# The last 64-slot expert pass stands step by step between the steps of the last 128-slot pass

## The chip, the cores and the metric

One core of a Trainium2 chip runs the whole kernel. The metric is device time in microseconds. A core has PE (the matrix engine, TensorE), DVE (VectorE), ACT (ScalarE), POOL (GpSimd) and SP (SyncE, which here only issues DMAs), and 16 DMA engines that bring data from HBM.

## What is computed

A two-layer encoder trunk on 256 tokens of 1024 columns, all float32. Layer 0 is dilated attention and a dense SwiGLU; layer 1 is grouped-query attention and a top-2-of-8 mixture of experts. The change touches the mixture alone:

```python
def moe_swiglu(h, router_w, w_gate, w_up, w_down):
    logits = (h @ router_w).astype(jnp.float32)
    top_val, top_idx = lax.top_k(logits, TOP_K)
    top_w = jax.nn.softmax(top_val, axis=-1)
    gates = jnp.sum(jax.nn.one_hot(top_idx, N_EXPERTS, dtype=jnp.float32) * top_w[..., None], axis=-2)
    y = jnp.zeros_like(h)
    for e in range(N_EXPERTS):
        y = y + gates[..., e:e + 1] * swiglu(h, w_gate[e], w_up[e], w_down[e])
    return y
```

`w_gate` and `w_up` are 1024 x 3584 for each expert, `w_down` is 3584 x 1024: 42 MiB an expert, 336 MiB in all, each byte fetched once.

## The kernel before, in words

**Passes.** Experts are ordered by how many tokens chose them. Each is a pass over its own slots: the tokens of an expert are gathered into 64 or 128 columns by a product with a 0/1 matrix, go through the SwiGLU, and are scattered back to the 256 tokens, weighted, by a product with the turned gate matrix (`SgT`). `PASSES` has six passes before the loop: five with 64 slots, kind S (places 0, 2, 3, 4, 5, here S0, S2 to S5), and the wide one, kind L (place 1, 128 + 64 slots). Two passes with 128 slots, kind M, follow: the one in a loop (here M6; the loop runs `loops` times, once with this data) and the last (here M7). Place 5 is the last S.

**Steps and tiles.** A pass has NF = 7 steps of 512 hidden columns. A step has six tiles of 1 MiB: two of gate weights, two of up, two of down. M7.2 is step 2 of M7. The downs of a step are done one step later, so a step is: gates, turning of the step before's hidden values, ups, downs of the step before.

**Two ways to multiply.** In a 64-slot step (`gate_beside_up`, `down_halves`) the tiles are multiplied as they landed, in float32, with gate and up beside each other in the two column halves of the array. In 128-slot and wide steps a tile is split: ACT makes the rounded high part (`high`, into one of three `whi`), DVE the rest (`low`, `wlo`), and PE adds three fast products per block (`tile_products`; it waits for high, then for low). The hidden values are split in the same way (`hidden_high` on ACT, `hidden_low` on DVE).

**Order.** `units()` lists the steps up to M6: the seven steps of S0, then S2 to S5 with the parts G, U and D (gates, ups, downs) of the seven wide steps put in behind the S steps that `WIDE_AFTER` names. All engines follow this list, each in order; within an S step, `middles` and `lates` name what else stands before and behind the second gate/up pair: gathers, turned gates, and pieces. A piece is one quarter of a scatter, taken through bank 6 of PSUM and added to `yacc` by DVE. Those of S5 (`piece`, L1729) also hold the wide expert's two parts, from `SgTl`, `yea` and `yeb`. Then comes the loop (`expert_pass`), and `expert_pass(..., True)` for M7; its own scatter stands behind its last downs.

**DMA.** SP issues the tiles in the order of use. A tile waits until its buffer is free (`raw_free`): for a split tile when `low` is done (`lo_done`), for one taken whole when PE has used it (`w_used`). There are six buffers (`RAW`), and two more while `RING_OF_8` holds (in the mix of S and wide steps). In an M step the two down tiles are asked for in the order second, first, once the buffer of the second is free (`e_down`, L627):

```python
raw_free(s + 1 - RAW, rr)
for k in (1, 0):
```

Of the kernel before, what the change touches and what calls it, by code (L numbers as in the profile page):

```python
# [38 lines left out]
NE = 8  # L39
# [44 lines left out]
WIDE_AFTER = ((0, 1, 2), (4, 5, 6), (8, 9, 10), (12, 13, 14), (15, 16, 17), (18, 19, 20), (21, 22, 23))  # L84
# [17 lines left out]
UNITS = units()  # L102

# [19 lines left out]

def small(q, i):
# [4 lines left out]
def small_before(q, i):  # L129

    if i:
        return q, i - 1
    return (max(q - 1, 0) if q > 2 else 0, NF - 1) if q else None
# [17 lines left out]
def as_landed():  # L151

    whole = set()
    for n, unit in enumerate(UNITS):
# [3 lines left out]
        elif unit[0] == "M":  # L158
            whole.update((s + 4, s + 5))
    return whole  # L160
# [3 lines left out]
SPLIT = [s for s in range(tile_of(NE + 1, 0) + 6 * NF) if s not in WHOLE]  # L164
# [15 lines left out]
def in_buffers():  # L180

    last, came, earlier = {}, {}, {}
    for s in range(tile_of(NE + 1, 0) + 6 * NF):
# [17 lines left out]
def split_before(s):  # L201

    return s - SPL if s >= LOOPED else SPLIT[split_at(s) - SPL]
# [48 lines left out]
def build(nc, dram, out):  # L252
    ctx = ExitStack()
    with ctx:
# [88 lines left out]

        rw = sb("rw", [P, KC, NE])
# [131 lines left out]
        tail_hidden = sem("tail_hidden")  # L476
        tb_done = sem("tb_done")
# [69 lines left out]
        def _(sp):  # L547
# [123 lines left out]
            for unit in UNITS:  # L671
# [16 lines left out]
                else:  # L688
                    e_gate(chosen[q], i, s, 0)
                    e_up(chosen[q], i, s + 2, 0)  # L690
                    e_down_static(chosen[FIRST_M - 1], NF - 1, s + 4, True)
            sp.wait_ge(w_used, FIRST_TILE["M", FIRST_M, 0])
# [8 lines left out]
            expert_tiles(FIRST_M, e, None, NF * loops)  # L701
# [29 lines left out]
        def _(act):  # L731
# [327 lines left out]
            def small_step(n, q, i, middle=None):  # L1059
# [12 lines left out]
                if w is not None:  # L1072
# [3 lines left out]
                    act.activation(hhb[:, :, 0:HP], tail_h, ACT.Copy).then_inc(bhi_done, 1)  # L1076
                following = UNITS[n + 1]
# [33 lines left out]
            def expert_pass(q, p=0, final=False):  # L1111
                rr = NF * p
                aside = {}
                if not final:
                    aside[5] = lambda: evacuate_gathers(q + 1, 2, p)
                    aside[6] = lambda: high_again(p, tile_of(q, 6), rr)
                for i in range(1, NF):
                    step(q, i, (q, i - 1), rr, 5 if final and i == NF - 1 else 6, aside.get(i))
                if final:
                    hidden_high(NHALF + steps_a(q) + NF - 1 + rr)  # L1120
                    gate_row(3)
                    act.wait_ge(w_used, tile_of(q + 1, 0) + 2 + 6 * rr)
                else:
                    step(q + 1, 0, (q, NF - 1), rr)
# [1513 lines left out]
```

## Time and profile before

| | |
|---|---|
| median of 3 runs | 1679.59 us (1675.41 to 1681.35) |
| profiled execution | 1682.09 us, span 1680.4 us |
| PE busy | 1623.3 us, 97% |
| DVE, ACT busy | 891.2 us (53%), 682.7 us (41%) |
| DMA | 504.78 MB, mean 300 GB/s |
| granted TensorE clock, mean | 0.983 |
| experts | 741 to 1666 us of the span |

The page gives busy time by engine and groups of instructions by source line; PE's products overlap, so that each record is longer than the distance to the next one (0.39 us against 0.23 us for 512 columns). A step's length is therefore read from start to start. DMA shares are means over 16 engines and can read a little over 1.

### The profile page before, as it was taken

The numbers are of one execution on the slowest core, as the hardware profiler recorded it, in microseconds if no ns is written. First come the engines' busy times: TensorE is split into PE (matmuls) and PEld (weight loads), VectorE is DVE, ScalarE is ACT, GpSimd is POOL, SyncE is SP. The second block draws the span as 40 slices with busy tenths as digits, with TensorE's granted clock in tenths as the row PEclk, the third lists the DMA queues.
The fourth block names the chain that finished last, engine by engine and source line by source line (L and its number), as shares of the span: only waits on it lengthen the run. The fifth ranks groups of instructions, "written<-read, shape, count | busy, mean of one in ns | idle before, by whom it ended". The sixth has DMA issues, their size and how long they took to land.

```text
span 1680.4 us, 23999 instructions
## 1 busy us (share of the span) xinstructions
PE 1623.3 (97%) x9497; PEld 1176.6 (70%) x9497; DVE 891.2 (53%) x989; ACT 682.7 (41%) x823; POOL 50.2 (3%) x100
## 2 busy tenths in 40 slices
PE   5999999999999999999899999999999999999997
PEld 4999999789999977753454545555555545788785
DVE  5666667667776679521133223233323225888786
ACT  2444445553333356520221322222232314667674
POOL 0200000001111000000000000000000000000000
PEclk9999999999999999979999999999999999999999
DMA  9986556248888633059999999999999999989993
GB/s 347 349 258 226 192 198 220 71 154 308 306 298 303 230 115 133 30 212 368 398 394 399 396 378 398 390 398 387 383 362 367 398 385 378 384 329 330 367 354 126
DMA packets 236641, 504.78 MB, mean 300 GB/s; under 512 B 11360, under 2 KB 83200, under 8 KB 227584
## 3 DMA queue, kind: packets, MB, share of 16 engines
q1 hardware_dynamic: 221264, 458.26, 74.6%
q0 software_dynamic: 12032, 43.00, 7.1%
q10 hardware_dynamic: 3248, 2.17, 0.4%
q8 instruction: 68, 1.11, 0.3%
q14 instruction: 29, 0.24, 0.0%
HBM read 502.34 MB, written 1.05 MB: 300 GB/s over the span
## 4 chain that ended last, share of the span: by engine, by line
PE 88%; DVE 5%; DMA 3%; ACT 2%; issue 1%; ACTq 0%; SPq 0%; DVEq 0%
PE ps L1618 15%; PE ps L1567 14%; PE ps L1168 10%; PE ps L1172 9%; PE ps L1175 9%; PE ps L1571 8%; PE ps L1631 7%; PE ps L1549 2%; PE ps L1655 1%; PE ps L1740 1%; PE ps L1261 1%; PE ps L1223 1%; DMA raw<-l_exp_w_up 1%; DVE wlo L1925 1%; DMA raw<-l_exp_w_down 1%
## 5 line engine op out<-in xcount | busy, mean ns | idle before, releaser
L1925 DVE TENSOR_TENSOR wlo<-raw,whi 128x2048 fp32r<-128x2048 f32 x210 | 476.7, 2288 | 221.3 <-ACT whi L740 216.7
L740 ACT ACTIVATE whi<-raw 128x2048 fp32r<-128x2048 f32 x210 | 398.9, 1910 | 147.0 <-PE ps L1172 80.5
L1168 PE MATMUL ps<-ahi,whi 128*128 128x256 f32 x832 | 239.1, 287 | 1.7 <-DVE alo L1993 1.7
L1172 PE MATMUL ps<-alo,whi 128*128 128x256 f32 x832 | 236.2, 284 | 0.0
L1175 PE MATMUL ps<-ahi,wlo 128*128 128x256 f32 x832 | 236.0, 284 | 0.0
L1618 PE MATMUL ps<-raw,arena 128*64 128x512 f32 x768 | 179.2, 610 | 7.4 <-DMA raw<-l_exp_w_up 5.3
L1168 PEld LDWEIGHTS ps<-ahi,whi 128*128 128x128 f32 x832 | 160.3, 193 | 5.1 <-issue 3.8
L1172 PEld LDWEIGHTS ps<-alo,whi 128*128 128x128 f32 x832 | 160.5, 193 | 0.3
L1175 PEld LDWEIGHTS ps<-ahi,wlo 128*128 128x128 f32 x832 | 160.4, 193 | 0.0
L2499 DVE TENSOR_TENSOR arena<-arena,ps 128x256 f32<-128x256 f32 x35 | 14.7, 421 | 273.9 <-ACT arena L1051 273.9
L1567 PE MATMUL ps<-whi,alo 128*128 128x512 f32 x448 | 156.6, 390 | 0.0
L1567 PE MATMUL ps<-whi,ahi 128*128 128x512 f32 x336 | 135.3, 403 | 0.0
L1618 PEld LDWEIGHTS ps<-raw,arena 128*64 128x64 f32 x768 | 53.1, 139 | 111.5 <-issue 106.4
L1168 PE MATMUL ps<-whi,ahi 128*128 128x256 f32 (+1 forms) x352 | 109.5, 311 | 2.5 <-DVE alo L1993 2.5
L1172 PE MATMUL ps<-whi,alo 128*128 128x256 f32 (+1 forms) x352 | 107.2, 305 | 0.0
L1175 PE MATMUL ps<-wlo,ahi 128*128 128x256 f32 (+1 forms) x352 | 107.1, 304 | 0.0
L1051 ACT ACTIVATE arena<-ps 128x256 f32<-128x256 f32 x35 | 13.4, 382 | 227.0 <-PE ps L1655 227.0
L1571 PE MATMUL ps<-wlo,ahi 128*128 128x512 f32 x336 | 103.6, 390 | 0.0
L1631 PE MATMUL ps<-raw,arena 128*64 128x512 f32 x448 | 101.6, 595 | 0.0
L1567 PEld LDWEIGHTS ps<-whi,alo 128*128 128x128 f32 x448 | 84.2, 188 | 18.0 <-issue 1.0
L1938 DVE SCALAR_TENSOR_TENSOR acc<-mod_raw,ccol,acc 128x1024 f32<-128x1024 f32 x70 | 89.6, 1280 | 0.9
L1567 PEld LDWEIGHTS ps<-whi,ahi 128*128 128x128 f32 x336 | 63.1, 188 | 27.1 <-issue 10.8
(296 smaller groups left out, 2333.2 us busy)
## 6 DMA issues: line engine op xcount, KB each, us to landing
raw<-l_exp_w_down SPq DMA_DIRECT2D x96, 1024.0 KB, 9.5
raw<-l_exp_w_up SPq DMA_DIRECT2D x88, 1024.0 KB, 11.0
raw<-l_exp_w_gate SPq DMA_DIRECT2D x86, 1024.0 KB, 9.3
raw<-l_w_in SPq DMA_DIRECT2D x42, 1024.0 KB, 6.5
mod_raw<-mod_w POOLq DMA_DIRECT2D x80, 512.0 KB, 5.8
mod_raw<-l_exp_w_gate SPq DMA_DIRECT2D x23, 1024.0 KB, 8.5
dist_gb<-l_exp_w_up SPq DMA_DIRECT2D x22, 1024.0 KB, 10.7
raw<-l_ffn_w_gate SPq DMA_DIRECT2D x14, 1024.0 KB, 5.1
```

What stands on the lines that cost most here:

```text
L740: act.activation(whi[n % SPL][:, :], landed_in(s), ACT.Copy).then_inc(hi_done, 1)
L1168: pe.matmul(dst, stat[0], mov[0], start=start, stop=False, skip_group_check=True)
L1172: hi = pe.matmul(dst, *cross[0], start=False, stop=False, skip_group_check=True)
L1175: return pe.matmul(dst, *cross[1], start=False, stop=stop, skip_group_check=True)
L1223: ins = pe.matmul(bank(b, kc, kc + 1), acc[:, kc * P:(kc + 1) * P], ones[:, 0:1], start=True, stop=True)
L1549: ins = pe.matmul(ps[:, b * BANK + kc * n:b * BANK + (kc + 1) * n], xo[:, tt, kc * P:(kc + 1) * P], sel[:, tt, :], start=(tt == 0), stop=( ...
L1567: ins = pe.matmul(dst, stat, whi[n % SPL][:, a:a + BANK], start=start, stop=False, skip_group_check=True)
L1571: ins = pe.matmul(dst, stat, wlo[n % SPL][:, a:a + BANK], start=False, stop=stop, skip_group_check=True)
L1618: ins = pe.matmul(half_bank(1, half), slots_of(q)[:, kc, :], landed_in(s + half)[:, kk * BANK:kk * BANK + BANK], start=kc == 0, stop=kc == ...
L1631: ins = pe.matmul(half_bank(0, half), sb_h[:, fc, :], landed_in(s)[:, at:at + BANK], start=i == 0 and fc == 0, stop=i == NF - 1 and fc == ...
L1925: dve.tensor_tensor(wlo[n % SPL][:, :], landed_in(s), whi[n % SPL][:, :].bitcast(F32), ALU.subtract).then_inc(lo_done, 1)
L1938: dve.scalar_tensor_tensor(acc[:, :], src, c, acc[:, :], ALU.mult, ALU.add).then_inc(mod_used, 1)
```

## The change

1. S5 leaves the list of units. S2 to S4 are followed by M6 at once, and `WIDE_AFTER` packs the wide parts behind the steps of three passes: the wide step 4's downs (D) and the wide step 5's gates (G) stand behind the same S step. The middles and lates are dealt out anew.
2. M7 becomes `final_pass`: a list FINAL with M7.1, S5.0, M7.2, S5.1, ..., M7.6, S5.5, then the downs of M7.6 (D), S5.6 and the downs of S5.6 (E). S5 computes in banks 3 and 2. The pieces that hold the wide expert now also hold M6's scatter and stand in S5.1 and S5.2. M6 scatters S4.
3. At the end the scatter products of M7 stand before the last downs of S5, and those of S5 (64 rows each, from `last_SgT` and `last_ye` in `mod_raw`) behind them, into the same four banks.
4. Eight buffers hold for 192 tiles instead of 240. From M6 on there are six, as before.

```diff
-WIDE_AFTER = ((0, 1, 2), (4, 5, 6), (8, 9, 10), (12, 13, 14), (15, 16, 17), (18, 19, 20), (21, 22, 23))
+LAST_S = 5
+WIDE_AFTER = ((0, 1, 2), (3, 4, 5), (6, 7, 8), (9, 10, 11), (12, 13, 14), (14, 15, 16), (17, 18, 19))
...
-    for n in range(NF * (FIRST_M - 2)):
+    for n in range(NF * (LAST_S - 2)):
...
+FINAL = [u for i in range(1, NF) for u in (("M", i), ("S", i - 1))] + [("D", NF - 1), ("S", NF - 1), ("E", NF - 1)]
...
-RING_OF_8 = range(AHEAD.stop, AHEAD.stop + 8 * 30)
+RING_OF_8 = range(AHEAD.stop, AHEAD.stop + 8 * 24)
...
+                if kind == "M":
+                    raw_free(EARLIER[s + 5], rr)
+                    for k in (1, 0):
+                        sp.dma_start(landed_in(s + 4 + k).rearrange("p (k n) -> p k n", k=2),
+                                     rows_256(e, i - 1, k, False)).then_inc(landed[buffer_of(s + 4 + k)], 16)
...
+                    if kind == "M":
+                        high(s + 3, rr)
+                        silu(f + i, s + 2 + 6 * rr)
+                        high(s + 4, rr)
+                        hidden_high(f + i - 1)
+                        high(s + 5, rr)
+                    if kind == "S":
+                        if i:
+                            small_silu(LAST_S, i - 1)
...
+                        act.wait_ge(w_used, s + 4 + 6 * rr)
+                        act.activation(sb_g, bank(3), ACT.Copy).then_inc(gu_copied, 1)
...
+                        for j in range({"M": SPL, "D": 2}.get(following[0], 0)):
+                            high(FINAL_TILE[following] + j, rr)
+                small_silu(LAST_S, NF - 1)
+                act.wait_ge(w_used, TILES + 6 * rr)
+                act.activation(last_ye[0:HP, :], half_bank(2, 0), ACT.Copy).then_inc(last_out, 1)
...
+                middles = {1: lambda: joint_piece(0), 2: lambda: joint_piece(2), 3: last_gates, 5: last_hidden}
+                lates = {1: lambda: joint_piece(1), 2: lambda: joint_piece(3), 5: lambda: spread_gate(3)}
...
+                    elif kind == "S":
+                        if i:
+                            pe.wait_ge(gu_copied, small(LAST_S, i))
+                        gate_beside_up(LAST_S, s, 0, 3, rr)
+                        if i:
+                            beside_T(small(LAST_S, i))
+                        if i in middles:
+                            middles[i]()
+                        gate_beside_up(LAST_S, s + 2, 1, 3, rr)
+                        if i in lates:
+                            lates[i]()
+                        if i:
+                            small_downs(LAST_S, i - 1, s + 4, 2, rr)
...
+                for j in range(4):
+                    pe.matmul(sums[j], SgT[:, j // 2 * P:j // 2 * P + P], ye[:, j % 2 * BANK:j % 2 * BANK + BANK],
+                              start=True, stop=False, skip_group_check=True)
+                small_downs(LAST_S, NF - 1, FINAL_TILE["E", NF - 1], 2, rr)
+                pe.wait_ge(last_out, 2)
+                for j in range(4):
+                    rows = slice(j % 2 * HP, j % 2 * HP + HP)
+                    pe.matmul(sums[j], last_SgT[rows, j // 2 * P:j // 2 * P + P], last_ye[rows, :],
+                              start=False, stop=True, skip_group_check=True).then_inc(scat, 1)
...
-            expert_pass(FIRST_M, loops, True)
-            pe.wait_ge(y_add, 4 * (FIRST_M - 1 + loops) + 1)
-            scatter(FIRST_M + 1, 0, 2, loops)
-            pe.wait_ge(gb_done, 4)
-            scatter(FIRST_M + 1, 1, 4, loops, False)
+            final_pass(loops)
```

Three places show how instructions now stand. DVE between the wide steps 4 and 5, before: low halves of two down tiles, four adds of wide sums, the hidden values of the next 64-slot step, a copy of turned gates, then the low halves of the next two wide tiles.

```order
L2514 TENSOR_TENSOR hhb<-mod_raw,hhb 128x4x64
L1925 TENSOR_TENSOR wlo<-raw,whi 128x2048 x2
L2491 TENSOR_TENSOR arena<-arena,ps 128x512 x4
L2499 TENSOR_TENSOR arena<-arena,ps 128x256
L2483 COPY arena<-ps 128x256
L1925 TENSOR_TENSOR wlo<-raw,whi 128x2048 x2
```

The same place after:

```order
L2648 TENSOR_TENSOR hhb<-mod_raw,hhb 128x4x64
L2057 TENSOR_TENSOR wlo<-raw,whi 128x2048 x2
L2625 TENSOR_TENSOR arena<-arena,ps 128x512 x4
L2057 TENSOR_TENSOR wlo<-raw,whi 128x2048 x2
L2633 TENSOR_TENSOR arena<-arena,ps 128x256
```

The 64-slot step that stood between the adds and the next gates' low halves stands behind them.

ACT in M7, around the end of a step, before: silu of the gates (L911), high parts (L740) and the hidden values' high part (L915).

```order
L534 REGISTER_ALU [waits w_used]
L911 ACTIVATE arena<-ps 128x512 [waits h_ready]
L534 REGISTER_ALU [waits landed4]
L740 ACTIVATE whi1<-raw4 128x2048 [waits lo_done,hi_used]
L914 REGISTER_ALU
L915 ACTIVATE hhi<-ps 128x512 [waits t_done]
L534 REGISTER_ALU [waits landed5]
L740 ACTIVATE whi2<-raw5 128x2048 [waits lo_done,hi_used]
L737 REGISTER_ALU
L534 REGISTER_ALU [waits landed0]
L740 ACTIVATE whi0<-raw0 128x2048 [waits lo_done,hi_used]
```

After, at the end of an M step and in the S step behind it (L1104 is the S step's silu, L1195 the copy of its gates):

```order
L968 ACTIVATE hhi<-ps 128x512 [waits t_done]
L559 REGISTER_ALU [waits landed3]
L793 ACTIVATE whi2<-raw3 128x2048 [waits lo_done,hi_used]
L1104 ACTIVATE arena<-ps 128x256 [waits tb_done]
L1194 REGISTER_ALU
L1195 ACTIVATE arena<-ps 128x512 [waits w_used]
L790 REGISTER_ALU
L559 REGISTER_ALU [waits landed4]
L793 ACTIVATE whi0<-raw4 128x2048 [waits lo_done,hi_used]
```

The high part of the next M step's first tile now stands behind the copy of the S step's gates, which waits for PE (`w_used`).

SP in M7, a step's ups and downs and the next step's gates, before:

```order
L563 DMA raw2<-l1_exp_w_up 128x4x512 [waits lo_done]
L534 REGISTER_ALU
L563 DMA raw3<-l1_exp_w_up 128x4x512 [waits lo_done]
L534 REGISTER_ALU
L632 ISA [waits lo_done]
L632 DMA raw5<-l1_exp_w_down 128x2x1024
L632 ISA
L632 DMA raw4<-l1_exp_w_down 128x2x1024
```

After, M7.2, the step behind S5.0:

```order
L588 DMA raw5<-l1_exp_w_gate 128x4x512
L576 REGISTER_ALU
L588 DMA raw0<-l1_exp_w_up 128x4x512 [waits w_used]
L576 REGISTER_ALU
L588 DMA raw1<-l1_exp_w_up 128x4x512 [waits w_used]
L576 REGISTER_ALU
L746 ISA [waits w_used]
L746 DMA raw3<-l1_exp_w_down 128x2x1024
L746 ISA
L746 DMA raw2<-l1_exp_w_down 128x2x1024
```

The buffers of these tiles came free with a split before; now they come free when PE has used the S step's tiles.

## Rows read from the trace of the kernel before

**Rows 1.** Busy by stretch: us; PE, PEld, DVE, ACT, POOL busy; clock; DMA share, GB/s.

```profile
859.10:1407.20 548.10, 548.10 (x2533) 280.53 (x2532) 160.31 (x198) 139.47 (x179) 0.00 (x0) 1.00 1.02 387
1407.20:1441.10 33.90, 32.48 (x146) 24.41 (x145) 26.19 (x16) 22.98 (x18) 0.00 (x0) 1.00 0.98 372
1441.10:1549.20 108.10, 108.10 (x499) 88.61 (x498) 92.49 (x60) 77.33 (x57) 0.00 (x0) 1.00 0.93 343
1549.20:1569.90 20.70, 18.63 (x77) 14.95 (x76) 15.60 (x9) 13.81 (x10) 0.00 (x0) 0.92 1.01 381
1569.90:1665.60 95.70, 95.67 (x435) 77.70 (x434) 77.80 (x50) 63.06 (x42) 0.00 (x0) 1.00 0.79 296
```

**Rows 2.** Waits of PE, 859 to 1666 us: us in total, times, longest.

```profile
PE ps L1567 <- DVE hlo L2125: 3.5, 2, 2.1
```

**Rows 3.** DMA in the mix, 800 to 1120 us.

```profile
DMA packets 49432, 125.84 MB, mean 393 GB/s; under 512 B 1918, under 2 KB 1918, under 8 KB 45318
```

**Rows 4.** Timeline of PE, a 64-slot step: start, us, engine, line.

```profile
1351.11 0.75 PE L1655 MATMUL ps<-cst,arena 128*128 128x128 f32 x4
1351.79 3.65 PE L1618 MATMUL ps<-raw,arena 128*64 128x512 f32 x16
1355.27 3.60 PE L1631 MATMUL ps<-raw,arena 128*64 128x512 f32 x16
1358.71 3.60 PE L1618 MATMUL ps<-raw,arena 128*64 128x512 f32 x16
1362.24 0.74 PE L1655 MATMUL ps<-cst,arena 128*128 128x128 f32 x4
```

**Rows 5.** Timeline of PE, the same place in two 128-slot steps running.

```profile
1520.98 0.60 PE L1398 MATMUL ps<-cst,arena 128*128 128x128 f32 x4
...
1537.82 0.60 PE L1398 MATMUL ps<-cst,arena 128*128 128x128 f32 x4
```

**Rows 6.** Chain that ended last, M6.1: start us, us, what.

```profile
1422.74 0.37 SPq L632
...
1423.31 6.92 DMA raw<-l_exp_w_down
...
1430.38 0.05 ACT whi L740
...
1435.55 1.65 PE ps L1567 x6
```

**Rows 7.** The same chain, M7.1.

```profile
1550.10 7.34 DMA raw<-l_exp_w_down
...
1562.79 3.42 PE ps L1567 x8
```

**Rows 8.** Stretches behind three holes of PE: columns as in rows 1.

```profile
802.50:808.00 5.50, 5.50 (x20) 2.02 (x21) 0.00 (x0) 0.00 (x0) 0.00 (x0) 0.73 1.05 402
1435.60:1440.00 4.40, 4.40 (x20) 3.62 (x20) 4.40 (x3) 2.69 (x2) 0.00 (x0) 1.00 1.05 387
1562.80:1567.20 4.40, 4.40 (x12) 3.48 (x13) 4.40 (x3) 1.75 (x2) 0.00 (x0) 0.61 1.06 390
```

**Rows 9.** Instructions by line and form: busy us, mean ns; idle before.

```profile
L1925 DVE TENSOR_TENSOR wlo<-raw,whi 128x2048 fp32r<-128x2048 f32 x119 | 268.7, 2287 | 97.1 <-ACT whi L740 97.1
L740 ACT ACTIVATE whi<-raw 128x2048 fp32r<-128x2048 f32 x119 | 225.5, 1912 | 52.5 <-PE ps L1567 37.7 <-DMA raw<-l_exp_w_gate 5.4 <-DMA raw<-l_exp_w_up 4.5
...
L1071 ACT ACTIVATE arena<-ps 128x512 f32<-128x512 f32 x35 | 20.9, 596 | 118.1 <-PE ps L1618 118.1
...
L2491 DVE TENSOR_TENSOR arena<-arena,ps 128x512 f32<-128x512 f32 x24 | 15.4, 683 | 24.3 <-PE ps L1582 15.6 <-PE ps L1588 8.7
```

**Rows 10.** Chain at the end, behind the last downs.

```profile
1665.57 1.16 issue
1666.73 3.69 PE ps L1707 x8
```

**Rows 11.** Timeline of ACT, a half-height copy.

```profile
1424.48 0.59 ACT L1057 ACTIVATE arena<-ps 64x512 f32<-64x512 f32 x1
```

More of the change, by code:

```diff
@@ L121, in tile_of, with final_tiles @@
     return FIRST_TILE["M", FIRST_M, 0] + 6 * (NF * (q - FIRST_M) + i)
+def final_tiles():
+    at, s = {}, tile_of(FIRST_M + 1, 1)
+    for unit in FINAL:
+        at[unit] = s
+        s += 2 if unit[0] in "DE" else 4 if unit == ("S", 0) else 6
+    return at, s
+FINAL_TILE, TILES = final_tiles()
 def small(q, i):
@@ L182, in in_buffers @@
     last, came, earlier = {}, {}, {}
-    for s in range(tile_of(NE + 1, 0) + 6 * NF):
+    for s in range(TILES):
         b = buffer_of(s)
@@ new lines, in final_pass, with joint_add, last_gates @@
+            def final_pass(loops):
+                rr, f = NF * (loops - 1), NHALF + steps_a(FIRST_M) + NF * loops
+                def joint_add(j, b):
+                    tt, n = j % 4 // 2, j % 2
+                    dve.wait_ge(y_add, 13 + 4 * loops + j)
+                    dve.wait_ge(scat, 12 + 4 * loops + j + 1)
+                    part_y = yacc[:, tt, n * BANK:n * BANK + BANK]
+                    dve.tensor_tensor(part_y, part_y, b, ALU.add).then_inc(y_add, 1)
+                def last_gates():
+                    dve.wait_ge(selT, FIRST_M + 1 + loops)
+                    dve.tensor_copy(SgT, bank(6, 0, NT * P)).then_inc(selT_e, 1)
+                middles = {1: lambda: joint_add(0, bank(6)), 2: lambda: (joint_add(2, bank(6)), choose(loops, True)),
+                           3: last_gates, 5: lambda: hidden_low(f + NF - 1, bank(6))}
+                lates = {1: lambda: joint_add(1, bank(6)), 2: lambda: joint_add(3, bank(6))}
+                for n, unit in enumerate(FINAL):
+                    (kind, i), s = unit, FINAL_TILE[unit]
+                    if kind == "M":
+                        low(s + 3, rr)
+                        low(s + 4, rr)
+                        hidden_low(f + i - 1, bank(6))
+                        low(s + 5, rr)
+                        hidden(f + i, s + 4 + 6 * rr)
+                    elif kind == "S":
+                        if i:
+                            small_hidden(LAST_S, i - 1)
+                        if i in middles:
+                            middles[i]()
+                        if i in lates:
+                            lates[i]()
+                        following = FINAL[n + 1]
+                        for j in range({"M": SPL, "D": 2}.get(following[0], 0)):
+                            low(FINAL_TILE[following] + j, rr)
+                small_hidden(LAST_S, NF - 1)
+                dve.wait_ge(w_used, TILES + 6 * rr)
+                dve.tensor_copy(last_ye[HP:P, :], half_bank(2, 1)).then_inc(last_out, 1)
+                for j, b in enumerate((4, 5, 0, 1)):
+                    joint_add(4 + j, bank(b))
```

275 lines of the change are left out of this document (168 added, 107 removed).

## The prediction, written before the changed kernel ran

> **What bounds the kernel now.** I read the stretches first, then the waits, then single steps. From 859 us to 1407 us (the mix: 64-slot passes S2 to S5 with the wide expert) PE is busy for 548.10 of 548.10 us, at full clock, while DMA moves 387 GB/s; in the next 258 us (the two 128-slot passes, M6 in the loop and M7 behind it) PE is full but for two holes, and DMA falls to 343 and 296 GB/s [rows 1]. The list of PE's waits over both says the same: two waits, 3.5 us in all, the longer 2.1 us [rows 2]. So PE's product stream sets the time from 859 to 1666 us, and DMA is close behind it in the mix: 393 GB/s is what it moves when it is always full [rows 3], which makes 2.67 us of a 1.049 MB tile, 16.0 us of the six tiles of a step.
>
> Two periods matter. A 64-slot step takes PE 11.13 us (transposes to transposes, 1351.11 to 1362.24: 0.68 transposes, 3.48 second gate/up pair, 3.44 downs, 3.53 first pair of the next step) [rows 4]. A 128-slot step takes 16.84 us (1520.98 to 1537.82) [rows 5]. Against 16.0 us of DMA the one eats DMA's lead and the other just keeps it.
>
> **What the change can't give.** The listing of PE's instructions holds the same products in the same shapes, in another order: 7 steps of S5 and the four three-part pieces leave the mix and stand in M7, the scatter of M7 stands ahead of the last downs instead of behind. PE is the full engine on both sides, so moving is worth nothing by itself; only holes in PE count. The change wins what holes it closes and loses what it opens.
>
> **The old holes stay.** The 1.4 us hole is in M6's second step. Its chain: the pair of down tiles is asked for at 1422.74, when the 64-slot downs free their buffers, the tile that is used first lands second at 1430.23, it is split, the hidden values' low half waits behind that on VectorE, and PE starts at 1435.55 [rows 6]. The 2.1 us hole is the same chain at the loop's end: 7.34 us from issue to landing, products at 1562.79 [rows 7]. Neither edge is touched by the change (S4 stands where S5 stood). What each holds: about 7.5 us from the request of a down pair to the landing, 5.3 us from the landing to PE's downs. Behind the second hole the granted clock reads 0.61 over 4.4 us (a part at 1.2 instead of 2.4 GHz), 1.7 us lost; behind the first it stays at 1.00; behind an earlier hole, at 802 us, it reads 0.73 over 5.5 us [rows 8]. I take 1.7 us for holes of 2.1 us and more, nothing for shorter ones.
>
> **New holes, one by one.** (Mk.i is step i of a 128-slot pass, Sk.i of a 64-slot pass.)
>
> 1. *Wide step 4 runs straight into wide step 5's gates.* PE waits for VectorE to add all four wide sums; after the last downs two adds of 0.683 us are left [rows 9], with 0.2 us of handing over: 1.6 us, once. Between 0 (if the adds were done) and 2.8 us (all four late); I take 1.6. Clock stays.
>
> 2. *S5.0 into M7.2.* ScalarE stands in order: it copies the gates of the 64-slot step (0.60 us) and only then makes the high half of the next 128-slot tile (1.91 us) [rows 9]. In every other 64-slot step small downs (3.44 us) cover this. S5.0 has none, so PE waits 0.60 + 1.91 + 0.1 = 2.6 us, then 0.4 us more for VectorE's low half (2.29 us against eight high products, 1.8 us). With the clock's 1.7: 4.7 us. Bounds 2.6 and 4.7.
>
> 3. *S5.1 into M7.3, S5.2 into M7.4.* The down pair of the 128-slot step may be asked for only when the 64-slot downs before it end; that is the hole of rows 6 again, 1.4 us each: 2.8 us, clock kept. The two pieces of 2.7 us in these steps give DMA time.
>
> 4. *S5.3 into M7.5, S5.4 into M7.6.* Here the queue itself is late. With six buffers (the mix has eight) nothing can be fetched ahead until the first gate/up pair of the 64-slot step is used; then six tiles must come, 16.0 us, and the one that is used first comes last, 2.0 us of latency on top (7.34 less two tiles) and 0.3 us to issue: landed 18.3 us after the pair, PE's downs ready 5.3 us later, at 23.6. PE's own way from there: 0.68 + 3.48 + 3.44 to the end of the 64-slot step, then 11.4 us to the 128-slot downs (16.84 less 5.44 of downs), 19.0 us in S5.4; the transposes of the last gates make it 19.4 in S5.3. Holes of 4.6 and 4.2 us, each with 1.7 us of clock: 12.2 us. Lower bound: the same at 403 GB/s and no clock loss, 8.0; upper, at 375 GB/s, 14.
>
> 5. *Entry to M6* is fetched in the last steps of S4 with six buffers, and the gather for M6 stands one step closer to it: ScalarE and VectorE finish about as PE arrives. 0.2 us, between 0 and 1.5.
>
> 6. *The end.* Before, PE stood 1.16 us after the last downs for a copy of 1024 columns, then did four scatter products in 3.69 us [rows 10]. Now the copy is half as high and half as wide, 0.59 us on each of two engines [rows 11], 0.71 with handing over: 0.45 us gained. The four products are as many, with 64 rows each. I take no gain of them (0 to 1.8 us).
>
> The Trainium skill, TensorEngine Tiling, section Overview, has it that products contracting 64 rows can run side by side in two halves of the array. For column halves the trace shows it: 16 records of half width end in 3.65 us. For row halves no run here shows it; by that rule the end would be half of 3.69 us, 1.8 us, shorter.
>
> What hides the rest: routing, choosing and gate work that moves on VectorE and ScalarE lies in the mix, where VectorE is busy for 160 and ScalarE for 139 of 548 us [rows 1]. SyncE's one more register load falls where it waits for a buffer.
>
> **Sum.** 1.6 + 4.7 + 2.8 + 12.2 + 0.2 - 0.45 = +21.0 us. The profiled execution took 1682.09 us, its span 1680.4 and 1.7 around it; it would take 1703.1. It lies 2.5 us above the median of the three runs, 1679.59; from the median the sum gives 1700.6, so 1701.
>
> **Rivals.**
>
> *DMA's lead carries (no change).* The mix now has three light 64-slot steps to each wide step where it had four, so DMA gets further ahead in it, and if M7 starts with all buffers full and the down pairs land in time, items 3 and 4 vanish. Left are 1.6 + 2.6 + 0.4 (no clock loss) - 0.45 - 0.5 = +3.7 us: 1683. Against it: a lead is capped by six buffers, and rows 6 show the hole right behind a full mix.
>
> *PE isn't the bound (faster).* If PE's busy share only hid waiting for data, DMA would be the bound, and filling it in the 128-slot passes would pay. The bytes there, 372 x 33.9 + 343 x 108.1 + 381 x 20.7 + 296 x 95.7, are 85.9 MB, at 393 GB/s 219 us instead of 258 [rows 1, 3]: up to 40 us, 1640. It decides at the first step where PE is full and could start earlier. Against it: PE's steps have the same length with DMA at 387 and at 296 GB/s, and nobody is named in its waits. A smaller form of it (the two old holes close, 3.5 + 1.7 us, and the end gives 2) lands at 1674.
>
> The Trainium skill, Perfetto Trace Analysis, section Identifying the Most-Contended Engine, holds matmul busy time to be a bad measure and wants the weight loads' share; the section Optimization Strategy says that interleaving regimes with different bounds may help. Weight loads are busy for 281 of 548 us in the mix and 89 of 108 us in M6 [rows 1]; by that rule PE has headroom in the mix and this rival holds, 1640 to 1674. I follow the rows on PE's waits.
>
> *M7 is bound by DMA all through (slower still).* If DMA's round trips leave each of the five edges from a 64-slot into a 128-slot step as item 4 has it, items 3 grow from 1.4 to 6.3 us each: +31 us, 1711. It decides when the pieces of S5.1 and S5.2 don't lengthen the way enough: 2 x 2.7 us against a hole of 4.6, so they should.
>
> **Chances and numbers.** The forecast 0.72 (its own range 1690 to 1709: no clock losses and 403 GB/s at one end, 375 GB/s and the late entry at the other); lead carries 0.10; faster 0.09; bound by DMA throughout 0.09. A measurement of this kernel tells about 0.3%, 5 us, from no change. Faster 0.09, same 0.10, slower 0.81. The range takes in the forecast and the case that the lead carries: 1683 to 1710.
>
> **What would show it.** In the changed kernel's trace: PE's steps of 11.1 and 16.8 us as before; a hole of about 1.6 us where wide downs meet wide gates; a wait of PE for the high half, some 2.6 us, after the 64-slot step that has no downs; then waits for the hidden values' low half, short ones in M7.3 and M7.4, 4 us in M7.5 and M7.6, each led by the landing of a down tile, with DMA near 393 GB/s across M7. I am wrong if PE's product stream in the mix gets shorter than its steps add up to (then it wasn't the bound), if the holes of M6.1 and M7.1 are gone (the lead does carry), or if M7.5 and M7.6 show none.

## The result and the profile of the changed kernel

| | kernel before | changed kernel |
|---|---|---|
| time, median of the runs side by side | 1679.99 us (4 runs) | 1705.72 us (4 runs, 1702.80 to 1709.61) |
| ratio to before | | 1.0163, 95% interval 1.0143 to 1.0182 |
| profiled execution, its span | 1682.09, 1680.4 us | 1702.80, 1701.1 us |

The change costs 25.7 us (1.6%). The forecast was 1701 in a range of 1683 to 1710, slower with a chance of 0.81. The sign and the size came out (the sum was 21.0 us), the size in part by luck: some of its terms were wrong, in opposite directions, and offset each other.

The page of the changed kernel, busy time by engine:

```profile
span 1701.1 us, 24069 instructions
PE 1625.0 (96%) x9497; PEld 1172.5 (69%) x9497; DVE 890.6 (52%) x986; ACT 680.5 (40%) x822; POOL 50.2 (3%) x100
```

The same stretches as in [rows 1]: the mix, M6, M7.1, and M7.2 to the end of the last downs, by each engine's busy time, granted clock, DMA share and GB/s:

```profile
851.50:1312.30 460.80, 459.42 (x2144) 249.26 (x2144) 154.34 (x187) 130.86 (x163) 0.00 (x0) 1.00 0.96 362
1312.30:1459.80 147.50, 143.10 (x645) 114.64 (x644) 119.43 (x75) 101.20 (x75) 0.00 (x0) 0.98 0.96 354
1459.80:1476.90 17.10, 17.10 (x79) 13.66 (x77) 11.68 (x7) 8.72 (x7) 0.00 (x0) 1.00 1.04 393
1476.90:1686.80 209.90, 194.66 (x823) 110.45 (x822) 85.39 (x58) 74.17 (x59) 0.00 (x0) 0.97 0.92 346
```

DMA now moves 346 GB/s where M7 moved 296 before, and nothing came of it: PE has 15 us of holes in that stretch. PE's waits from 860 us to the end of the downs name them (us in total, times, longest), where [rows 2] had two waits and 3.5 us:

```profile
PE ps L1646 <- DVE hlo L2257: 16.9, 6, 4.6
PE ps L1646 <- ACT whi L793: 2.5, 1, 2.5
PE ps L1646 <- DVE arena L2625: 1.4, 1, 1.4
PE ps L1650 <- DVE wlo L2057: 0.2, 1, 0.2
```

L1646 and L1650 are the 128-slot products (L1567 and L1571 before), L2257 makes the low half of the hidden values, L793 the high half of a weight tile, L2625 adds the wide sums. Stretch by stretch, measured from PE's start of a step to its start of another:

| stretch | before | after | difference |
|---|---|---|---|
| start to the mix (S0, S1, routing) | 838.39 | 830.82 | -7.6, not by the change |
| mix, to M6.0 | 568.89 | 481.50 | -87.4 |
| M6, to M7.1 | 141.93 | 147.46 | +5.5 |
| M7.1 | 20.73 | 17.09 | -3.6 |
| M7.2 to the end of the downs | 95.63 | 209.96 | +114.3 |
| end | 14.83 | 14.27 | -0.6 |

The first line holds none of the changed code; it varies between executions (24 us at the lower clock around 724 us in the one profile, 3.4 in the other). From the mix on the change costs 28.2 us in these two profiles. The medians of the whole time differ by 25.7, and the two spans alone (20.7 apart) would have told a story that is too short.

### The profile page after: what moved, and what is told of

Same layout as the page of the kernel before. It is cut to its first block, busy times and chain, and to the rows that moved or that the text cites. A ratio compares the mean times of both kernels' runs of the same rounds, so it can differ in the third digit from the quotient of the medians.

```text
span 1701.1 us, 24069 instructions
## 1 busy us (share of the span) xinstructions
PE 1625.0 (96%) x9497; PEld 1172.5 (69%) x9497; DVE 890.6 (52%) x986; ACT 680.5 (40%) x822; POOL 50.2 (3%) x100
## 2 busy tenths in 40 slices
DMA packets 236643, 504.78 MB, mean 297 GB/s; under 512 B 11361, under 2 KB 83201, under 8 KB 227585
## 4 chain that ended last, share of the span: by engine, by line
PE 85%; DVE 5%; DMA 5%; ACT 2%; issue 2%; SPq 0%; ACTq 0%; DVEq 0%
PE ps L1697 14%; PE ps L1646 13%; PE ps L1247 10%; PE ps L1251 9%; PE ps L1254 9%; PE ps L1650 7%; PE ps L1710 7%; DMA raw<-l_exp_w_down 3%; PE ps L1628 2%; PE ps L1734 1%; PE ps L1340 1%; PE ps L1302 1%; ACT whi L793 1%; DMA raw<-l_exp_w_up 1%; DVE wlo L2057 1%
## 5 line engine op out<-in xcount | busy, mean ns | idle before, releaser
L2057 DVE TENSOR_TENSOR wlo<-raw,whi 128x2048 fp32r<-128x2048 f32 x218 | 495.1, 2289 | 245.2 <-ACT whi L793 240.2
L793 ACT ACTIVATE whi<-raw 128x2048 fp32r<-128x2048 f32 x218 | 412.7, 1909 | 151.8 <-PE ps L1251 80.5
L1697 PE MATMUL ps<-raw,arena 128*64 128x512 f32 x720 | 165.6, 603 | 7.7 <-DMA raw<-l_exp_w_up 5.2
L1646 PE MATMUL ps<-whi,alo 128*128 128x512 f32 x448 | 156.8, 390 | 0.0
L1646 PE MATMUL ps<-whi,ahi 128*128 128x512 f32 x336 | 135.4, 403 | 3.9 <-ACT whi L793 2.5
L1697 PEld LDWEIGHTS ps<-raw,arena 128*64 128x64 f32 x720 | 49.1, 137 | 103.3 <-issue 98.7
L1710 PE MATMUL ps<-raw,arena 128*64 128x512 f32 x528 | 120.0, 596 | 0.0
L1104 ACT ACTIVATE arena<-ps 128x256 f32<-128x256 f32 x35 | 13.4, 383 | 242.2 <-PE ps L1734 242.2
L1650 PE MATMUL ps<-wlo,ahi 128*128 128x512 f32 x336 | 104.5, 392 | 0.2 <-DVE wlo L2057 0.2
L1646 PEld LDWEIGHTS ps<-whi,alo 128*128 128x128 f32 x448 | 84.2, 188 | 17.6 <-issue 0.5
L1697 PE MATMUL ps<-mod_raw,arena 128*64 128x512 f32 x192 | 87.4, 598 | 0.0
```

Of the source, the lines that this page charges most:

```text
L793: act.activation(whi[n % SPL][:, :], landed_in(s), ACT.Copy).then_inc(hi_done, 1)
L1646: ins = pe.matmul(dst, stat, whi[n % SPL][:, a:a + BANK], start=start, stop=False, skip_group_check=True)
L1650: ins = pe.matmul(dst, stat, wlo[n % SPL][:, a:a + BANK], start=False, stop=stop, skip_group_check=True)
L1697: ins = pe.matmul(half_bank(b, half), slots_of(q)[:, kc, :], landed_in(s + half)[:, kk * BANK:kk * BANK + BANK], start=kc == 0, stop=kc == ...
L1710: ins = pe.matmul(half_bank(b, half), sb_h[:, fc, :], landed_in(s)[:, at:at + BANK], start=i == 0 and fc == 0, stop=i == NF - 1 and fc == ...
L2057: dve.tensor_tensor(wlo[n % SPL][:, :], landed_in(s), whi[n % SPL][:, :].bitcast(F32), ALU.subtract).then_inc(lo_done, 1)
```

## The experiments

The theory by now: PE is the bound everywhere from the mix to the end, the products are conserved, and the 26 us are holes, each made by a tile or a copy that comes late, with the lower clock behind the long ones. The rivals: DMA sets the time in M7 and PE's busy share hides it; a hole that is closed is handed on (closing one opens the next); products in this order cost PE more by themselves.

**1. The down pair in the order of use.** Both down tiles of a 128-slot step wait for the second buffer, and the one used first is fetched second. The edit turns the pair round and, from the second step of a pass on, gives each tile its own wait (`downs` takes the rows in the same order; the loop's `e_down` is edited alike):

```diff
-                    raw_free(EARLIER[s + 5], rr)
-                    for k in (1, 0):
+                    if i == 1:
+                        raw_free(EARLIER[s + 5], rr)
+                    for k in (0, 1):
+                        if i > 1:
+                            raw_free(EARLIER[s + 4 + k], rr)
                         sp.dma_start(landed_in(s + 4 + k).rearrange("p (k n) -> p k n", k=2),
-                                     rows_256(e, i - 1, k, False)).then_inc(landed[buffer_of(s + 4 + k)], 16)
+                                     rows_256(e, i - 1, 1 - k, False)).then_inc(landed[buffer_of(s + 4 + k)], 16)
```

> The changed kernel, but in every 128-slot step the down tile that is used first is also fetched first, and from the second step of a pass on each of the two waits for its own buffer alone. Theory 'late pair' (the holes come from the down pair: asked for when the 64-slot downs end, the tile used first landing last): the tile used first lands 2.7 us earlier. The hole in M6.1 falls from 4.4 to about 1.7 us and its clock loss of 1.8 goes; the holes in M7.3 and M7.4 (1.5, 1.4) vanish; those in M7.5 and M7.6 fall from 4.6 and 4.5 to about 1.8 us without clock loss. In all 15 to 19 us less than the changed kernel: about 1689 us, within 0.6% of the kernel before. Rival 'bytes' (M7 is bound by DMA's rate as a whole, the order inside only shifts where PE waits): less than 4 us, 1702 or more, with holes of the same sum elsewhere in M7.

Measured: 1692.83 us (median of 5 runs), ratio 1.0086 (1.0056 to 1.0116), half of the loss gone. PE's waits over the same stretch:

```profile
PE ps L1652 <- ACT whi L799: 5.2, 3, 2.5
PE ps L1652 <- DVE hlo L2263: 5.2, 3, 1.9
PE ps L1652 <- DVE arena L2631: 1.4, 1, 1.4
PE ps L1656 <- DVE wlo L2063: 0.6, 3, 0.2
```

The waits for the hidden values' low half fall from 16.9 us to 5.2 (M6.1, M7.5 and M7.6, none over 1.9); those of M7.3 and M7.4 are gone. M7.2's 2.5 us stays, and M7.5 and M7.6 now also wait a little at their gates. So five of the holes were the late down pair. The time came out 4 us above the forecast, which had no room for those gate waits (2.7 us in the list) nor for what M6.1, M7.5 and M7.6 kept.

**2. The highs of M7.2 ahead of the copy.** ScalarE makes the high halves for M7.2 before it copies the gates of S5.0:

```diff
+                        following = FINAL[n + 1]
+                        if i == 0:
+                            for j in range(SPL):
+                                high(FINAL_TILE[following] + j, rr)
                         act.wait_ge(w_used, s + 4 + 6 * rr)
                         act.activation(sb_g, bank(3), ACT.Copy).then_inc(gu_copied, 1)
...
-                        following = FINAL[n + 1]
-                        for j in range({"M": SPL, "D": 2}.get(following[0], 0)):
+                        for j in range({"M": SPL, "D": 2}.get(following[0], 0) if i else 0):
```

> The changed kernel, but in S5.0 ScalarE makes the three high parts for M7.2 before it copies the 64-slot step's gates. Theory 'place in ScalarE's line': PE's wait for the high part at M7.2 (2.5 us, with 0.2 and 0.45 us of small waits behind it) vanishes, 3 us less than the changed kernel, about 1703 us; the holes behind it may grow by a part of that, since PE comes to them earlier. Rival 'tile late' (the gate tile of M7.2 has not landed): the wait stays at 2.5 us, now named by the DMA.

Measured: 1708.96 us (4 runs), ratio 1.0201 (1.0160 to 1.0243): no gain. The wait for the copy is gone from the list:

```profile
PE ps L1649 <- DVE hlo L2260: 20.9, 6, 4.8
```

But these waits have grown from 16.9 us to 20.9: PE's wait at M7.2's own downs was 0.5 us in the changed kernel and is 4.5 here (the 4.8 of the list is M7.5's). The chain that ended last there (start us, us, what):

```profile
1483.96 0.37 SPq L746
...
1484.82 9.75 DMA raw<-l_exp_w_down
...
1494.72 0.05 ACT whi L793
...
1499.77 3.77 PE ps L1649 x8
```

The down pair is asked for at the end of S5.0 in any case; PE reaches the downs 3 us earlier and waits there instead, long enough to get the lower clock (eight products in 3.77 us). M7.2's 2.5 us was a cover for the late pair. This is the second rival, "handed on", and for this one hole it holds. The time was forecast at 1703 us, since the hole behind was to grow by a part only.

**3. The kernel before with six buffers ahead of M6.** The loop (from M6.1 on) runs with six buffers. By the numbers in the code (`RING_OF_8.stop` against the first tile of the loop) the ring of eight ends 4 tiles ahead of it before the change and 10 ahead of it after; it can only be cut in pieces of 24 tiles, so the smallest cut in the kernel before puts its end 28 tiles ahead. The edit does that alone:

```diff
-RING_OF_8 = range(AHEAD.stop, AHEAD.stop + 8 * 30)
+RING_OF_8 = range(AHEAD.stop, AHEAD.stop + 8 * 27)
```

> The kernel before, but the two extra buffers end 24 tiles earlier, 22 tiles ahead of M6, so that the last steps before M6 have six buffers, as the changed kernel has them from 4 tiles ahead of M6. Theory 'six buffers at the entry' (M6.1's hole grew from 1.4 to 4.4 us because the tiles of M6.0 and M6.1 are asked for late): the hole in M6.1 grows to 3 us or more, with 1.7 us of clock, and PE may wait in S5 too: 4 to 12 us slower than the kernel before, 1684 to 1692 us. Rival 'gather and routing stand one step closer to M6' (a matter of the new order, not of buffers): the hole stays at 1.4 us, 1680 us.

Measured: 1685.08 us (10 runs), ratio 1.0036 (1.0017 to 1.0055). The chain of M6.1, where [rows 6] had 6.92 us from issue to landing:

```profile
1422.44 0.37 SPq L632
...
1423.00 10.61 DMA raw<-l_exp_w_down
...
1433.76 0.05 ACT whi L740
...
1438.92 3.35 PE ps L1567 x7
```

And of the changed kernel:

```profile
1327.78 0.37 SPq L657
...
1328.35 10.18 DMA raw<-l_exp_w_down
...
1338.68 0.05 ACT whi L793
```

The pair is asked for at the same place of PE's work and lands 3.3 to 3.7 us later, behind tiles that were asked for late. With six buffers SyncE can't ask for M6's tiles in time: in the changed kernel it issues nothing from 1292.3 to 1308.5 us:

```profile
1289.68 2.59 SPq L588 DMA_DIRECT2D raw<-l_exp_w_gate  x2
1308.46 0.93 SPq L588 DMA_DIRECT2D raw<-l_exp_w_up  x2
```

These are M6.0's up tiles, 3.9 us ahead of M6.0's first product. In experiment 3 they are asked for 3.9 us ahead of it too, in the kernel before 10.7 us. So six buffers ahead of M6 are enough to make this hole with all steps in their old order, and 5.5 of the 28 us are of this kind. The cut tested is longer than the change's (28 tiles for 10), and the size is the same, 4.4 us; that 10 alone do it is the reading of the queue, not a run.

**4. A seventh buffer from S5.0 on**, in the second half of the array that the ring of eight used:

```diff
+SEVEN = FINAL_TILE["S", 0]
...
     if s in AHEAD:
         return RAW + s - AHEAD.start
+    if s >= SEVEN:
+        turn = (s - SEVEN) % 7
+        return (SEVEN - 7 + turn) % RAW if turn else 2 * RAW - 2
...
```

> The changed kernel with a seventh buffer from S5.0 on, a half of mod_raw that is free there; the down pair is fetched in the old order. Theory 'late pair': the seventh buffer lets each tile be asked for one tile earlier: M7.3 and M7.4 lose their holes (the pair waits for a gate/up pair and the first small-down tile instead of the last), M7.5 and M7.6 lose 2.7 us each and their clock loss: 10 to 13 us less than the changed kernel, about 1694 us; M6.1 stays at 4.4 us. Rival 'bytes': M7's holes keep their sum, 1704 us.

Measured: 1701.44 us (4 runs, 1694.11 to 1704.16), ratio 1.0149 (1.0112 to 1.0186). The forecast of 1694 was missed: by time it can't be told from the changed kernel. Its trace (the run of 1694.11, the fastest of the four) shows part of the forecast: M7.3 and M7.4 have no hole, M7.6's shrinks to 2.5 us without low clock, but M7.5 keeps 4.1 us and its low clock. My reading, not tested, is that one buffer more is not enough for a queue that is six tiles behind.

**5. The order of use in the kernel before.** The edit of experiment 1 on the kernel before (`e_down` and `downs`):

```diff
-                raw_free(s + 1 - RAW, rr)
-                for k in (1, 0):
-                    src = dram["l1_exp_w_down"][bass.ds(e, 1), bass.ds(i * 512 + 256 * k, 256), :]
+                if i == 0:
+                    raw_free(s + 1 - RAW, rr)
+                for k in (0, 1):
+                    if i:
+                        raw_free(s + k - RAW, rr)
+                    src = dram["l1_exp_w_down"][bass.ds(e, 1), bass.ds(i * 512 + 256 * (1 - k), 256), :]
...
-                            fc, a = 2 * k + kk, kk * D + n * BANK
-                            first, last = i == 0 and fc == 0, i == NF - 1 and fc == 3
+                            fc, a = 2 * (1 - k) + kk, kk * D + n * BANK
+                            first, last = i == 0 and k == kk == 0, i == NF - 1 and k == kk == 1
```

> The kernel before, with one edit: in every 128-slot step the down tile that is used first is asked for first, each of the two as soon as its own buffer is free, where before both waited for the second buffer. Theory (the old holes are late down pairs): the tile that is used first lands 2.7 us and more earlier, the holes of M6.1 (1.4 us) and M7.1 (2.1 us and 1.7 us of clock) close, 5 us less: 1675 us, ratio 0.997. If the holes only shrink as that of M6.1 did in the changed kernel (from 4.4 to 1.9), half of it: 1677. Rival (the holes are set by VectorE's low half, however early the tile comes): 1680, both holes still in the trace.

Measured: 1673.90 us (12 runs) beside 1677.71 (23 runs of before), ratio 0.9978 (0.9961 to 0.9994). It is the one version here that beats both kernels, by 0.2%. All that is left in its list of PE's waits over the same stretch is the wait at the very end:

```profile
PE ps L1710 <- issue: 1.2, 1, 1.2
```

Both old holes and the low clock are gone (3.5 and 1.7 us by the profile; 3.8 us by the medians).

**6. The three edits together, in the changed kernel** (those of experiments 1, 2 and 4).

> The changed kernel with the three edits together: down pair in the order of use, the highs of M7.2 ahead of the copy of the gates, a seventh buffer from S5.0 on. Theory (every new hole is a late tile or a late copy, and nothing else was lost): from 1693 us with the pair order alone, M7.2's wait (2.5 us) and what was left at M7.5 and M7.6 (four short waits, some 4 us in all) close; the entry's 1.9 us and the wide sums' 1.4 us stay: 1686 us, ratio 1.004. Rival (a wait that is closed is handed on to the next late tile, as M7.2's was when it was closed alone): 1692 us or more. Rival 2 (products interleaved this way cost more on PE by themselves): holes gone, time still above 1695.

Measured: 1686.15 us (10 runs), ratio 1.0047 (1.0029 to 1.0066), the time that the theory had. PE's waits:

```profile
PE ps L1659 <- DVE hlo L2270: 4.5, 3, 1.9
PE ps L1659 <- DVE arena L2638: 1.4, 1, 1.4
PE ps L1659 <- ACT whi L803: 0.9, 1, 0.9
PE ps L1663 <- DVE wlo L2070: 0.2, 1, 0.2
```

7.0 us of waits are left, 3.5 more than in the kernel before, and it is still 8 us behind that by the medians, 7.1 from the mix on in the two profiles. So some 4 us are not in the list; they come up again below. The waits at M7.5 and M7.6 were to close and only shrank, from 6.4 us in experiment 1 to 3.8, so this part of the theory holds in part only. With the pair order in place the edit of experiment 2 does pay: M7.2 has no hole.

**7. The pair order and the seventh buffer only.**

> The changed kernel with the down pair in the order of use and the seventh buffer, without the edit at M7.2's highs. Theory (the three edits close different holes): M7.2's 2.5 us stay, the short waits at M7.5 and M7.6 go: 1689 us, 3 above the kernel with all three. Rival (the two edits close the same holes, so the second adds nothing to the first): 1693 us, as with the pair order alone.

Measured: 1688.76 us (4 runs), ratio 1.0080 (1.0053 to 1.0107), 2.6 above experiment 6, with M7.2's 2.5 us in the trace and 3.3 us of short waits still at M7.5 and M7.6. The intervals of the two overlap, so this rests on the trace.

**8. Less data for S5.** From S5.1 on, the gate and up tiles bring a quarter of their rows and the down tiles half:

```diff
+            def part(s, src, dims):
+                raw_free(EARLIER[s], rr)
+                sp.dma_start(landed_in(s).rearrange("p (k n) -> p k n", k=dims[0])[:, 0:1, :],
+                             src[:, 0:1, :]).then_inc(landed[buffer_of(s)], 16)
...
-                    if kind == "S":
+                    if kind == "S" and i:
+                        part(s + 2 * k, expert_half("l1_exp_w_gate", last, k, i * 512), (4, 512))
+                        part(s + 2 * k + 1, expert_half("l1_exp_w_up", last, k, i * 512), (4, 512))
+                    elif kind == "S":
...
-                        fetch(s + 4 + k, rr, rows_256(last, i - 1, k, True), (2, D))
+                        part(s + 4 + k, rows_256(last, i - 1, k, True), (2, D))
```

> The changed kernel, with less data for the steps 1 to 7 of S5 that stand in M7: each gate and up tile brings a quarter of its rows (the other rows keep what the buffer held) and each down tile half. The products and copies are as many as before; S5's output is not the reference's. Some 29 MB less is moved in M7, 75 us at 393 GB/s. Theory (PE is the bound and DMA sets only the holes): PE's steps keep their 11.1 and 16.8 us; the holes of M7.5 and M7.6 (4.6 and 4.5 us, 1.7 us of clock behind each) shrink to the 1.4 us that M7.3 and M7.4 have, since the down pair is still asked for when the 64-slot downs end, or go; M6.1 and M7.2 stay: 1696 us (1692 to 1698), ratio 1.010. Rival (DMA is the bound in M7 and PE's busy time hides it): the time falls by tens of us, to 1630 to 1660.

Measured: 1707.51 us (4 runs), ratio 1.0177 (1.0147 to 1.0208). Both forecasts were wrong. The pages of the two runs have 504.78 and 479.62 MB, so the edit takes out 25 MB, not the 29 of the expectation, and it gained nothing. PE's waits still have M7.5's and M7.6's holes:

```profile
PE ps L1654 <- DVE hlo L2265: 17.2, 6, 4.5
```

DMA around M7.5, in stretches of 4 us (columns as in [rows 1]):

```profile
1584.00:1588.00 4.00, 4.00 (x24) 1.59 (x20) 0.00 (x0) 0.13 (x1) 0.00 (x0) 1.00 0.02 4
1588.00:1592.00 4.00, 4.00 (x21) 1.42 (x22) 0.76 (x2) 0.54 (x2) 0.00 (x0) 1.00 0.85 286
1592.00:1596.00 4.00, 4.00 (x20) 1.62 (x17) 1.36 (x1) 2.81 (x3) 0.00 (x0) 1.00 1.05 389
1596.00:1600.00 4.00, 4.00 (x18) 2.94 (x17) 3.23 (x2) 3.21 (x2) 0.00 (x0) 1.00 1.06 394
1600.00:1604.00 4.00, 4.00 (x21) 3.30 (x20) 3.07 (x2) 2.45 (x3) 0.00 (x0) 1.00 1.03 409
1604.00:1608.00 4.00, 2.89 (x13) 2.06 (x11) 1.51 (x1) 1.67 (x1) 0.00 (x0) 1.00 0.96 358
1608.00:1612.00 4.00, 0.61 (x3) 0.54 (x4) 3.63 (x3) 2.53 (x3) 0.00 (x0) 1.00 0.05 13
```

DMA stands nearly still, at 4 GB/s, in the 4 us ahead of 1588, then is full for 18 us, then stands still again, while PE waits. Those 18 us are the 128-slot step's own six tiles, which none of the lightened tiles are; they can be asked for only when the 64-slot step's first pair gives its buffers free. What I had lightened was the wrong half. For the rival "DMA is the bound" the run is decisive all the same: with 25 MB less and DMA idle for whole stretches, the time stays.

**9. Less data for M7**, the mirror of it: the gate and up tiles of M7.2 to M7.6 bring a quarter of their rows, all else is whole.

```diff
-                        fetch(s + k, rr, expert_half("l1_exp_w_gate", e, k, i * 512), (4, 512))
+                        part(s + k, expert_half("l1_exp_w_gate", e, k, i * 512), (4, 512))
...
-                if kind == "M":
+                if kind == "M" and i > 1:
+                    for k in range(2):
+                        part(s + 2 + k, expert_half("l1_exp_w_up", e, k, i * 512), (4, 512))
+                elif kind == "M":
```

> The changed kernel, with less data for the 128-slot steps 2 to 7 of M7: each gate and up tile brings a quarter of its rows (the other rows keep what the buffer held), the down tiles are whole, S5's tiles are whole. The products and copies are as many as before; M7's output is not the reference's. It is the mirror of the run that lightened S5's tiles and left the holes of M7.5 and M7.6 as they were, with DMA full for just the 18 us of the 128-slot step's own six tiles (1588 to 1606 us there) and nearly idle ahead of them. Theory (the holes are the round trip of those six tiles, asked for only when the 64-slot step's first pair is used): with 4 of them at a quarter (0.67 us each for 2.67) the pair lands 7.5 us after the 64-slot downs end, as in M7.3; PE's holes at M7.5 and M7.6 shrink from 4.6 and 4.5 us to 1.4 or less and their low clock goes, M6.1 and M7.2 stay: 1697 us (1694 to 1699), ratio 1.011. Rival (the holes are set by the two down tiles alone, whatever comes ahead of them): holes of 4 us and more, 1704 to 1708 us.

Measured: 1693.10 us (6 runs, 1688.80 to 1700.88), ratio 1.0058 (1.0039 to 1.0077); its profiled execution is one of the longer ones, 1698.92. PE's waits:

```profile
PE ps L1654 <- DVE hlo L2265: 10.4, 5, 4.4
PE ps L1654 <- ACT whi L801: 2.5, 1, 2.5
```

The 4.4 is M6.1, which isn't touched. M7.5's hole is 2.1 us and M7.6's 1.3, where it was 4.6 and 4.5. The forecast was 1.4 or less and no lower clock for both; M7.5's is longer and keeps 3.4 us of it. The down pair before M7.5 now lands in 7.36 us instead of 10.21, and PE starts 12.6 us behind its issue:

```profile
1594.65 7.36 DMA raw<-l_exp_w_down
...
1607.23 2.98 PE ps L1654 x8
```

That is [rows 7]'s round trip again, so what is left is the late request, as in M7.3. The median lies 4 us under the forecast, the profiled execution 2 above it.

## Why the prediction was right

Its reading of the bound held. The mix became shorter by 87.4 us. By the prediction's own lengths, seven steps of 11.13 us and four pieces of 2.7 us leave it, 88.7, and a hole of 1.6 comes in: 87.1. PE's steps keep their length wherever no hole is in them, but for some 0.5 us a round in M7 (below). The rule on weight loads that it set against the rows, from the Trainium skill, Perfetto Trace Analysis, section Identifying the Most-Contended Engine, would have PE with headroom in the mix: the mix has loads busy for 249 of 461 us, and the time follows the matmuls there. The trace speaks against it in this kernel.

| term of the sum | predicted | measured |
|---|---|---|
| 1, wide step 4 into wide step 5 | 1.6 | 1.4 wait (1.3 by the mix's length) |
| 2, S5.0 into M7.2 | 2.6 + 0.4 + 1.7 of clock | 2.5 + 0.6, no clock |
| 3, M7.3 and M7.4 | 1.4 each | 1.5 and 1.4 |
| 4, M7.5 and M7.6 | 4.2 and 4.6, + 3.4 of clock | 4.6 and 4.5, + 5.2 of clock |
| 5, entry to M6 | 0.2 (0 to 1.5) | 5.5 |
| old hole of M7.1 | stays | gone, -3.6 |
| 6, end | -0.45 | -0.56 |
| not in the sum | | 3.3 in small gaps, some 2 that I can't place |

**Items 3 and 4** held in mechanism and size. The rows for M7.5 (start us, us, what):

```profile
1588.56 10.21 DMA raw<-l_exp_w_down
...
1603.98 3.78 PE ps L1646 x8
```

The first pair of S5.3 is used up at 1579.5. The prediction counts 18.3 us from there to the landing of the tile used first; it lands at 1598.8, 19.3 us later, and PE starts 5.2 us behind it (predicted 5.3). Experiments 1, 8 and 9 say why: the pair's order makes M7.3 and M7.4, the six tiles' way makes M7.5 and M7.6. Only the clock was undersized; the stretch behind M7.6's hole:

```profile
1639.70:1645.90 6.20, 6.15 (x15) 4.83 (x16) 2.72 (x2) 0.00 (x0) 0.00 (x0) 0.51 1.06 402
```

6.2 us at 0.51 cost 3.0 us and 4.5 us at 0.52 behind M7.5's hole 2.2, where the stretch behind M7.1's hole before [rows 8] cost 1.7.

**Item 2** has the right mechanism and one term too many. The 2.5 us for the high half are there, and no lower clock behind them:

```profile
1486.40:1490.00 3.60, 3.33 (x13) 2.43 (x14) 3.55 (x2) 3.60 (x4) 0.00 (x0) 1.00 1.05 406
```

**Item 5** is the step that failed: "ScalarE and VectorE finish about as PE arrives. 0.2 us". It names the six buffers and charges nothing for them (its 0.2 us are for the gather and the engines that split), though item 4 works out for M7 what six buffers do when a queue has to catch up. It is the same sum, at another place: M6.1's hole grows from 1.4 to 4.4 us and gets the lower clock, 2.4 us more:

```profile
1344.00:1349.00 5.00, 5.00 (x13) 3.94 (x13) 4.60 (x3) 2.02 (x2) 0.00 (x0) 0.52 1.04 344
```

Experiment 3 has it without any of the new order. The prediction's "S4 stands where S5 stood" was true of the steps and false of the ring.

**The hole of M7.1** was to stay ("Neither edge is touched by the change") and is gone, in the changed kernel and in every variant of it. The change does touch this edge. M7.1's up tiles and its down pair are asked for, before (M7.1 starts at 1549.21 us),

```profile
1543.09 3.16 SPq L563 DMA_DIRECT2D raw<-l_exp_w_up  x2
1549.55 0.93 SPq L632 DMA_DIRECT2D raw<-l_exp_w_down  x2
```

and after (M7.1 starts at 1459.78):

```profile
1448.00 2.56 SPq L588 DMA_DIRECT2D raw<-l_exp_w_up  x2
1456.46 0.93 SPq L746 DMA_DIRECT2D raw<-l_exp_w_down  x2
```

Counted from M7.1's start, the up tiles are asked for 5.7 us earlier and the pair 3.7, and ScalarE no longer waits 2.2 us for an up tile. The code has the reason. Before, M7's tiles are asked for by the function of M6's pass, with M6's tile numbers and all counts moved on by 42 tiles (`expert_tiles(FIRST_M, e, None, NF * loops)`). But the step ahead of M6.1 has four split tiles and two taken whole, and the step ahead of M7.1 has six split ones. So M7.1's up tiles wait for two more low halves than their buffers need, those of the down tiles ahead of them, and the pair waits until PE has used the tiles in its buffers, not only until they are split. `final_pass` has numbers of its own, and each tile waits for its own buffer. Experiment 3 has the old code and keeps the hole (1.9 us). This is read from the code and from the times of issue; no run has the kernel before with these waits alone put right. This miss and the clock of item 2 offset item 5 (3.6 and 1.7 us against 5.3), so the total came out better than its terms: that much of the hit was luck.

**What the sum lacked.** A round of a 64-slot and a 128-slot step has more than its two steps. Timeline of PE in the changed kernel, transposes of three 128-slot steps running:

```profile
1527.17 0.60 PE L1477 MATMUL ps<-cst,arena 128*128 128x128 f32 x4
1562.75 0.60 PE L1477 MATMUL ps<-cst,arena 128*128 128x128 f32 x4
1593.21 0.60 PE L1477 MATMUL ps<-cst,arena 128*128 128x128 f32 x4
```

The second round, 30.46 us, is 16.84 [rows 5] and 11.13 [rows 4], 0.31 for two routing products and 1.56 from the downs' hole, 29.84; 0.6 us is left. The first leaves 0.5. Six rounds make some 3.3 us. It is spread over products that follow a change of form (a 64-slot group of 16 takes 3.59 us from start to start for 3.48), no wait names it, and experiment 6 still has it: the first of these rounds has no hole there, takes 33.86 us (1526.41 to 1560.27), and leaves 0.4. At that rate six rounds make 2.4 of the 3.6 us by which experiment 6 is behind from the mix on with no wait to name them. That is the third rival of the experiments, small but there.

**Item 6** came out by two things that weren't in it. Products and adds at the end, by line:

```profile
L1994 PE MATMUL ps<-mod_raw 64*128 64x512 f32 x8 | 2.0, 615 | 0.8 <-DVE mod_raw L2732 0.8
L2702 DVE TENSOR_TENSOR arena<-arena,ps 128x512 f32<-128x512 f32 x4 | 2.7, 686 | 1.4 <-PE ps L1994 1.3
```

Eight products of 64 rows of 615 ns each are done in 2.0 us, where [rows 10] had eight full ones in 3.7: they run side by side, as the Trainium skill, TensorEngine Tiling, section Overview, says. But the 1.7 us don't reach the end, for VectorE's four adds of 0.69 us follow one another and now take longer than the products.

The rivals: "DMA's lead carries" fell, since all four holes of items 3 and 4 are there and the lead was the first thing that six buffers cut; "PE isn't the bound" fell with the mix's length and with experiment 8; "M7 is bound by DMA all through" fell, since M7.3 and M7.4 lose 1.5 us and not 6.

## What to carry to other kernels

When PE is full, moving its work to where DMA has room gains nothing, and what it costs can be read ahead: take each edge between two kinds of steps, and follow its tile from the moment its buffer comes free, through what is queued ahead of it, to the product that needs it. Do this at every place where the number of buffers changes, also where the steps themselves don't. Before closing a wait, see what arrives behind it: here one closed wait only showed the next, and the cheap edit that did pay was to fetch the tile that is used first first. Where one function fetches for several passes, check that its waits fit the steps ahead of each: M7.1's old hole was there for a count that fitted M6.

## What was not expected of the hardware

- The lower clock doesn't go by the length of a hole alone. Holes of 1.9 us (M6.1 in experiment 1) and 2.1 us (M7.5 in experiment 9) were followed by 3.4 us of it, those of 4.4 us and more by 3.4 to 6.8 us, while M7.2's 2.5 us had none in any of the six kernels that have it (the changed one, experiments 1, 4, 7, 8 and 9).
- It doesn't go by the place of the hole, nor by the kind of products ahead of it. M7.1's hole was 2.1 us in the kernel before, with 3.4 us at the lower clock behind it, and 1.9 us in experiment 3, with none. Ahead of M7.2's hole PE did 32 products with 64 slots; it did as many ahead of the 3.3 us hole that ends at 802.5 us in the kernel before, and that one is followed by the lower clock there (0.73 over 5.5 us, [rows 8]) and by none in the profiled executions of experiments 1 and 7 (1.00). What decides it, no run here tests.
- DMA has its rate again at once when it is asked (experiment 8): 4 GB/s in the 4 us ahead of 1588 us, then 286, 389 and 394 GB/s in the next three stretches of 4 us.
